# Three transformer layers on one core: a thin output projection two groups to a bank, and a second block with its values first

## What is computed

```python
# first block, after its first attention and residual:
h = rms_norm(x, norm_xattn);  m = rms_norm(mem, norm_mem)
q = (h @ xattn_wq)            # 4 heads of 128
s = softmax(q k^T / sqrt(128));  o = s v                # k, v from m
x = x + o @ xattn_wo          # 512 -> 2048: only 4 k-tiles of 128
h = rms_norm(x, norm_mlp)
x = x + square(relu(h @ w_up)) @ w_down
# second block, for l in range(2):
h = rmsnorm(x, norm_mix)
proj = h @ w_in               # qa ka va | qb kb vb | qc kc vc
oa = window_attention(qa, ka, va, sink, t5_table)       # 8 heads of 64
ob = neighborhood_attention(qb, kb, vb, b_rpb)          # 8 heads of 64, a bias and a mask
oc = axial_global_attention(qc, kc, vc, gains)          # 16 heads of 64, rotary
mix = concat(rmsnorm(oa), rmsnorm(ob), rmsnorm(oc))
x = x + mix @ w_o
h = rmsnorm(x, norm_mlp)
x = x + square(relu(h @ w_up)) @ w_down
```

## Time and profile before

| | |
|---|---|
| median of 3 runs | 3400.99 us (3398.97 to 3401.2) |
| the profiled execution | 3402.23 us, its span 3400.4 us |
| mean granted TensorE clock | 0.993 |
| PE busy | 98% of the span |
| DVE, ACT, POOL busy | 63%, 48%, 28% |

### The profile page before, as it was taken

One profiled execution on the slowest core, in us unless ns is written; L12 is line 12 of the kernel. 1 busy time (PEld: TensorE's weight loads), 2 busy tenths in 40 slices (PEclk: granted clock), 3 DMA queues, 4 the chain that ended last, 5 costly groups with the idle time before them and its releaser, 6 DMA issues.

```text
span 3400.4 us, 49070 instructions
## 1 busy us (share of the span) xinstructions
PE 3328.1 (98%) x19306; PEld 2885.9 (85%) x19306; DVE 2144.3 (63%) x3029; ACT 1635.9 (48%) x2755; POOL 948.4 (28%) x891
## 2 busy tenths in 40 slices
PE   8999998999999999999999999999999999999998
PEld 7888787888888887788888888888788888888887
DVE  5657566664576556777775467655777776457654
ACT  4455454443444544555444344444654544344443
POOL 1433132220132223246321023222336422013222
PEclk9999999999999999999999999999999999999999
DMA  6544453755555553465555555555354555555554
GB/s 215 194 152 143 138 172 131 251 191 197 184 189 191 190 189 127 140 177 165 186 184 188 193 186 191 194 186 175 122 172 158 186 186 188 196 186 188 197 186 142
DMA packets 187276, 605.58 MB, mean 178 GB/s; under 512 B 36485, under 2 KB 41461, under 8 KB 187046
## 3 DMA queue, kind: packets, MB, share of 16 engines
q1 hardware_dynamic: 187046, 602.44, 53.6%
HBM read 600.13 MB, written 8.00 MB: 179 GB/s over the span
## 4 chain that ended last, share of the span: by engine, by line
PE 88%; DVE 5%; ACT 4%; issue 1%; POOL 1%; DMA 0%; SPq 0%; POOLq 0%; DVEq 0%; ACTq 0%
PE ps L1591 87%; DVE wl L2171 3%; ACT wh L1926 2%; PE ps L1594 1%; DVE sS L2175 1%; ACT sS L2022 1%; ACT tA L1926 0%; ACT x L1926 0%; ACT sS L2011 0%; ACT sS L1988 0%; POOL acc L2505 0%; POOL sS L2505 0%; ACT tS L1931 0%; ACT ua L1926 0%; DVE den L2313 0%
## 5 line engine op out<-in xcount | busy, mean ns | idle before, releaser
L1591 PE MATMUL ps<-x,wh 128*128 128x512 f32 x4880 | 1735.1, 399 | 18.5 <-DVE x L2179 13.8
L2171 DVE TENSOR_TENSOR wl<-wt,wh 128x1024 fp32r<-128x1024 f32 x1098 | 1453.4, 1357 | 281.7 <-ACT wh L1926 266.8
L1591 PE MATMUL ps<-x,wl 128*128 128x256 f32 x4880 | 1370.9, 281 | 0.0
L1926 ACT ACTIVATE wh<-wt 128x1024 fp32r<-128x1024 f32 x1098 | 1108.2, 1052 | 173.4 <-PE ps L1591 162.6
L1591 PEld LDWEIGHTS ps<-x,wh 128*128 128x128 f32 x4880 | 919.6, 188 | 237.2 <-DVE wl L2171 14.7
L1591 PEld LDWEIGHTS ps<-x,wl 128*128 128x128 f32 x4880 | 925.9, 190 | 0.4
L1591 PE MATMUL ps<-ua,wh 128*128 128x512 f32 (+1 forms) x2432 | 844.2, 392 | 20.2 <-DVE xr L2171 9.3
L2171 DVE TENSOR_TENSOR tB<-ps,tA 128x256 f32<-128x256 f32 x497 | 208.8, 423 | 845.5 <-ACT tA L1926 843.6
L1926 ACT ACTIVATE tA<-ps 128x256 f32<-128x256 f32 x497 | 188.1, 382 | 1071.7 <-PE ps L1591 1062.7
L1591 PE MATMUL ps<-ua,wl 128*128 128x256 f32 x2368 | 666.1, 281 | 0.0
L1591 PEld LDWEIGHTS ps<-ua,wh 128*128 128x128 f32 x2432 | 455.0, 189 | 124.7 <-issue 10.0
(11 more groups left out here) (231 smaller groups left out, 1659.4 us busy)
## 6 DMA issues: line engine op xcount, KB each, us to landing
wt<-in_w_up SPq DMA_DIRECT2D x384, 512.0 KB, 3.9
wt<-in_w_down SPq DMA_DIRECT2D x384, 512.0 KB, 4.5
wt<-in_w_in SPq DMA_DIRECT2D x202, 512.0 KB, 4.4
wt<-in_w_o SPq DMA_DIRECT2D x64, 512.0 KB, 4.2
wt<-in_w_out SPq DMA_DIRECT2D x32, 512.0 KB, 4.2
wt<-in_wkv SPq DMA_DIRECT2D x16, 512.0 KB, 4.3
wt<-in_cw SPq DMA_DIRECT2D x8, 512.0 KB, 4.6
wt<-in_wq SPq DMA_DIRECT2D x8, 512.0 KB, 4.4
```

The costliest lines, as they stand in the source:

```text
L1591: return eng.matmul(o, l, r, start=start, stop=stop, skip_group_check=True)
L1926: return eng.activation(o, i, ACT.Copy, **kw)
L2171: return eng.tensor_tensor(o, a, b, op)
```

## The change

1. In the thin projection a group holds two outputs, one in each half of a bank: 4 groups of 4 tiles to a unit in place of 8 of 2. DVE adds 128x512 to two outputs of `xr` at once (`x = xr[:, o:o + 2, :]`), and `more` runs for both behind it.
2. `unit` gets `stages`, the values of `n` at which the background goes on: (3, 10, 15) and (7, 13) in the last two units of `xattn_wq`, (8, 13) and (4, 11) in the units of the thin projection.
3. In the second block vc comes before kc, and within B the order is qb, kb, vb. B's pairs are started together with A's. A pair waits for its values before their product, no longer before the scores. A takes slots 8 to 11 and B 12 to 15 (the rows of `w_o` are swapped on the host).
4. The factors of C's norm come at `n == 3` of the second unit of `w_o` (`across`), not right behind the first; until then evictions are held.

```diff
-ORDER2 = [26, 27, 28, 29] + [18 + i for i in range(8)] + [4, 5, 0, 1, 2, 3] + [6 + i + 4 * j for i in range(4) for j in (2, 0, 1)]
+ORDER2 = [28, 29, 26, 27] + [18 + i for i in range(8)] + [4, 5, 0, 1, 2, 3] + [6 + i + 4 * j for i in range(4) for j in range(3)]
...
-                if n == 8:
+                if n in stages:
                     run_deferred()
                     step_bg()
...
-    def at_once(begin, end):
+    def across(begin, end):
         kept = {}
 
         def first():
             kept["b"] = begin()
+            held["evac"] = True
+
+        def second():
+            end(kept["b"])
+            held["evac"] = False
+            run_pending()
         at13.append(first)
-        after_unit.append(lambda: end(kept["b"]))
+        after_unit.append(lambda: at3.append(second))
...
-        while (held["s1"] >= 1 or dens.spare() < 4 or not has("a_v", *v) or not (bias or sS.spare() >= 2)
+        while (held["s1"] >= 1 or dens.spare() < 4 or not (bias or sS.spare() >= 2)
...
+        while not has("a_v", *v):
+            yield
         av_heads(pr, [(hds[j], pts[j], j, v) for j in range(2)])
...
-        last_q = unit([(True, True, project("yq", i, "Q", free="yqfree"))], KT, X2)
+        last_q = unit([(True, True, project("yq", i, "Q", free="yqfree"))], KT, X2,
+                      stages=((8,), (8,), (3, 10, 15), (7, 13))[i])
...
-            last_p = unit([(True, True, residual("mlp", 8 * u + g, part == 1, G_MLP, thin=True, x2free=[last_q],
-                                                 last=(lambda: norm_T("mlp")) if 8 * u + g == 15 else None))
-                           for g in range(8)], 2, UA(2 * part), thin=True)
+            last_p = unit([(True, True, residual("mlp", 8 * u + 2 * g, part == 1, G_MLP, thin=True, x2free=[last_q],
+                                                 last=(lambda: norm_T("mlp")) if 8 * u + 2 * g == 14 else None))
+                           for g in range(4)], 4, UA(2 * part), thin=True, stages=(4, 11) if u else (8, 13))
...
-            slot = {"C": i, "B": 8 + i, "A": 12 + i}[br]
+            slot = {"C": i, "A": 8 + i, "B": 12 + i}[br]
...
-            elif 6 <= t < 10:
-                pair("B", t - 6)
             elif t == 5:
-                for i in range(4):
-                    pair("A", i)
+                for br in "AB":
+                    for i in range(4):
+                        pair(br, i)
...
-        gens = [spawn(branch("B", 1, 8)), spawn(branch("A", 2, 12))]
+        gens = [spawn(branch("A", 2, 8)), spawn(branch("B", 1, 12))]
...
-        at_once(lambda l=l: norm_begin((l, "C"), "accs0", "branch"), branch_end)
+        across(lambda l=l: norm_begin((l, "C"), "accs0", "branch"), branch_end)
...
-                    tt(xr[:, o, :], xr[:, o, :], ps[:, g % 3, 0:T], ALU.add).then_inc(S.v_sum)
+                    x = xr[:, o:o + 2, :]
+                    tt(x, x, ps[:, g % 3, :].rearrange("p (a b) -> p a b", a=2), ALU.add).then_inc(S.v_sum)
```

More of the change, by code:

```diff
@@ L249, in matmuls, with unit @@
             step("mm", h, k, k + 1)
-    def unit(parts, nk, src, thin=False):
+    def unit(parts, nk, src, thin=False, stages=(8,)):
         u = state["u"]
@@ L277, in unit @@
                 end = last and k == nk - 1
-                tiles[h].append((g, src(j, k), first and k == 0, end, thin))
+                if thin:
+                    half = 2 * k // nk
+                    tiles[h].append((g, src(j, k % (nk // 2)), k % (nk // 2) == 0, end, half))
+                else:
+                    tiles[h].append((g, src(j, k), first and k == 0, end, None))
                 matmuls(h, n % 8)
@@ L442, in ev @@
         def ev(g):
-            take("xw%d" % o, "xw", g)
+            os = (o, o + 1) if thin else (o,)
+            for i in os:
+                take("xw%d" % i, "xw", g, i)
             if thin:
@@ L455, in ev, with both, more @@
                 give(("tB", b), t)
-            give("xw%d" % o, t)
+            for i in os:
+                give("xw%d" % i, t)
             if not final:
                 return None
[L460 to L482, removed]
+            if thin:
+                def both():
+                    more(o, t)
+                    more(o + 1, t)
+                return both
+            return lambda: more(o, t)
+        def more(o, t):
+            step("more", st, o, nxt, fold)
+            p.free[("xw", st, o)] = [t]
+            if nxt is not None:
+                p.free[("x2", st, o)] = x2free
+                tick("a_x2hi", st, o)
+                tick("v_x2", st, o)
+                give("xr_split%d" % o, ("v_x2", at["v_x2", st, o]))
+            if fold:
+                take("rM", "rM", st, o)
+                square(st, o, "fold")
+            if o == 0:
+                take("acc", "acc", st)
+            if o == KT - 1 and not fold:
+                take("tS", "tS", st, o)
+                tick("a_sq", st, o)
+            else:
+                square(st, o)
+            if nxt is None:
+                give("xw%d" % o, tick("a_fin", o))
+            if last and o == KT - 1:
+                last()
         return ev
@@ L1599, in weights @@
                 for k in range(k0, k1):
-                    g, (src, i, key), start, end, thin = tiles[h][k]
+                    g, (src, i, key), start, end, half = tiles[h][k]
                     bank, c = ps[:, g % 3, :], slice(k * P, (k + 1) * P)
-                    if start:
+                    if start and not half:
                         let_go(w, "bank", g)
@@ L1609, in weights @@
                         x = U2(i)
-                    if thin:
-                        mm(bank[:, 0:T], wh[h % 4][:, c], x[:, 0:T], start, False)
-                        mm(bank[:, 0:T], wh[h % 4][:, c], x[:, T:2 * T], False, False)
-                        m = mm(bank[:, 0:T], wl[h % 4][:, c], x[:, 0:T], False, end)
+                    if half is not None:
+                        o = bank[:, half * T:half * T + T]
+                        stop = tiles[h][k][3] or k < 7 and tiles[h][k + 1][2]
+                        mm(o, wh[h % 4][:, c], x[:, 0:T], start, False)
+                        mm(o, wh[h % 4][:, c], x[:, T:2 * T], False, False)
+                        m = mm(o, wl[h % 4][:, c], x[:, 0:T], False, stop)
                     else:
@@ L2358, in _ @@
                     w.wait_ge(by_name[name], n)
-                    let_go(w, "xw", g)
-                    tt(xr[:, o, :], xr[:, o, :], ps[:, g % 3, 0:T], ALU.add).then_inc(S.v_sum)
+                    let_go(w, "xw", g, o)
+                    let_go(w, "xw", g, o + 1)
+                    x = xr[:, o:o + 2, :]
+                    tt(x, x, ps[:, g % 3, :].rearrange("p (a b) -> p a b", a=2), ALU.add).then_inc(S.v_sum)
                 elif kind == "memsplit":
```

4 lines of the change are left out of this document (2 added, 2 removed).

## The result

The changed kernel takes 3386.59 us (median of 5 runs, 3385.87 to 3390.24) against 3398.97 for the kernel before beside it (5 runs, 3393.34 to 3401.2): a ratio of 0.9967, interval 0.9953 to 0.9982. It is faster, by 12.4 us where 21.4 were forecast.

The account below looks back on a forecast made before the run. PE bounds the kernel (busy 3328.1 of 3400.4 us), so time comes off only its waits and low clock. Gains 5.3 + 3.6 + 7.9 + 4.6 = 21.4 give 3380; range 3376 to 3385, chance 0.60.

Parts of the forecast that it names:

- rivals A: Last thin part keeps most of its time: part 1's net gain nil, `w_up` stall 2 longer, about 3386; chance 0.15.
- rival B: Clock falls elsewhere, at `vturn` or in `w_o`, so the 5.1 credited to it is lost: 3385; chance 0.12.
- Part 0, 5.3: Head steps between `xattn_wq` matmuls: 4.7 of waits and 0.9 of slowed starts go, 0.3 charged; gain 5.3.
- Part 1, 3.6 net: Thin projection, two outputs a bank: 18.4 against 22.9, gain 4.5, minus 0.9 in the first unit of `w_up`.
- The bound on the squares: POOL's sums of squares beside DVE's splits in the thin projection: up to 3 us if POOL held ACT; not summed.
- Second block, the heads of both layers: Stalls of 1.72 and 1.77 in layer 0, 1.0 and 0.9 in layer 1 go; 0.5 added for vc's copy.
- The clock term of 3.4: Second block, layer 0: low clock of two windows, 1300 to 1310 and the ten us behind, removed: 2 x 1.7.
- 5.1 us credited to the clock: Second block, both layers: low clock goes with the gaps of 1.7 us, called a guess about cause; 5.1.
- The additions of layer 1: Second block, layer 1: the same three charges as layer 0 (0.5, 0.4, 0.9), given as 1.9 in all.
- one more case in which a turn stands right behind another pair's turn: Second block: a further late `sP`, as at 1438.12 where it came 1.26 late; charged 0.9.
- Rival D: Slower: PE waits on B's masks, 3.90 each, eight in full 31.2, giving 3411; chance 0.02.
- The removal of the `ua` waits: Before `w_o`: 2.0 in layer 0, 2.1 in layer 1 go through C's factors at `n == 3` and B's later-read slots.

Follow-up runs that it names:

- second_only: The kernel before with only the second block's plan of the change (parts 3 and 4): ratio 0.9994 (0.9986 to 1.0003) to the kernel before.
- b_spawn_old: The changed kernel with B's pairs started one by one with their own query unit, as before: ratio 0.9989 (0.9978 to 1.0000) to the kernel before.

## Why the prediction was right, and where it was not

**The sign and the range** were right; the size was 1.7 times too large. The 3386.6 lies outside the 3376 to 3385 that had 0.60, where rivals A and B stand (3386 and 3385). A did not come: the last part of the projection took 18.36 us for 18.4 forecast. B did, as told below.

**Part 0, 5.3.** The sum up to `w_up` was right (9.8 forecast, 10.6 measured), and so were its stages: 5.95 in `xattn_wq` and part 0 (5.3 forecast), 4.7 in part 1 (4.5 forecast). Which edit gives what was not. The term took all 4.7 us of waits for the head steps. 2.6 of them waited for `xr`, and those went with the longer evictions: part 2 is worth 2.8, part 1 of the change 7.8.

**Part 1, 3.6 net.** The cadence of 2.36, the wait of 3.76 before the last group (forecast: about 4), the low clock behind it and the stall in `w_up` all came. In `w_up` the price depends on when `sink` lands: 1.4 and 2.1 against 0.9. The unit took 11.6 us as forecast (11.4), but before it had taken 9.4, not 10.5. The wait for `x` in it was put at about 4; it was 1.90 in one execution and 4.44 in the other.

**The bound on the squares** was in the right place: DVE's low halves take 0.62 each where they took 0.51, and the squares' one buffer paces bunched outputs. No wait of PE names it, but ACT waits for POOL's sum nine times between 529 and 551 us, 0.43 to 1.12 each, where before it waited twice in that part (0.95 and 0.83). Before the add that frees the last group's bank (`xr<-xr,ps` at 536.89) DVE waits 0.20 and 0.60 for ACT's halves, so that up to 0.8 us of the 3.76 is this:

```profile
535.06 0.66 DVE L2203 SCALAR_TENSOR_TENSOR x<-xr,par,x 128x256 fp32r<-128x256 f32 x1 [0.20 <-ACT x L1950]
536.32 0.65 DVE L2203 SCALAR_TENSOR_TENSOR x<-xr,par,x 128x256 fp32r<-128x256 f32 x1 [0.60 <-ACT x L1950]
536.89 0.68 DVE L2195 TENSOR_TENSOR xr<-xr,ps 128x512 f32<-128x512 f32 x1
```

**Second block, the heads of both layers.** 1.72, 1.77, 1.0 and 0.9 of waits went, and 0.56 for the copy of vc came, as forecast. The clock term of 3.4 was half a guess: the dip at 1300 went and in both executions of the changed kernel one came near 1270 to 1280, behind waits of 0.95 and 0.85 that the kernel before has too. In five of the ten other executions with the new order of kc and vc there was none, and the stretch took 186.8 to 186.9, the 5.7 us of gain (6.4 forecast). Both executions with the old order had two dips there. Over the whole second block, up to the end of its second `w_o`, the kernel before has 10.2 us at half the clock (three dips of 3.4), the changed kernel 10.2 in one execution and 6.8 in the other. So of the 5.1 us credited to the clock none came in the first execution and 1.7 in the second. That was rival B. (The additions of layer 1, "1.9 in all", are 1.8 by their three terms, which moves nothing.)

**Second block, B and `w_o`.** This is, with the clock, the step that failed: "one more case in which a turn stands right behind another pair's turn [...] say 0.9". It came, in both layers, at 2.68, and with the clock's dip the unit is 3.4 us too long (12.45 against 9.07 in layer 0; the stretch of layer 1's last seven units 56.00 against 52.60). The stall of 1.26 from which 0.9 was taken is one of A, with no mask; B's mask lengthens DVE's splits beside it (3.40 against 2.37). The prediction weighed DVE's splits beside POOL's work for the squares, and did not ask it of the masks, one of which the new order puts ahead of such a turn's copy. Rival D had the masks as a wait of PE for POOL; that never came. They cost through DVE.

**`w_o`** has two waits for a bank, 1.9 us, in which two evictions stand behind two splits and the work on a branch's slots of `ua`; only 0.4 was charged. They are there without part 4 too, and in the kernel before one of 0.32 stood in their place. The removal of the `ua` waits was right, the reason wrong: they stay away without the factors at `n == 3` and without the swap of slots. They also stay away without B's early start, where a wait of 3.0 for B's `den` comes first. Which piece removes them was not shown; what the runs show is that the early start saves that wait of 3.0.

The missing 9.6 us (21.4 less 11.8 in the first execution) are then: 3.0 in layer 0 and 4.1 in layer 1 for B and `w_o`, 2.3 and 0.5 in the heads, 0.5 in `w_up`, less 0.8 gained above forecast. These numbers hold the 5.1 us of the clock. What part of a dip comes by chance is open: two executions of one kernel differ by 2.8 us in one stretch.

## What to carry to other kernels

Between a turn and its partner there must be more work than the copy's own engines have in their queues: count what stands ahead of the copy on ACT, and what DVE must do before that, in that unit, not in the one where such a stall was last seen. A new order moves the small steps between the products too: ask of each, a mask here, whether it comes to lie beside DVE's two-input work. And where outputs are bunched, look for the single buffer (`tS` here) that ties three engines into one cadence. Last, before a term is credited to the clock, look at more than one execution: here the dips came back elsewhere.

## What the hardware showed

PE ran full-clock stretches without waits at one of two tile rates, 0.347 or 0.353 us for two matmuls (5.55 or 5.65 us a unit), in the long stretches constant from the second unit on. Which one was drawn anew in each execution: the last 27 units of the first `w_up` took 149.8 in five and 152.6 in nine of 14 profiled executions, the second block's 179.2 or 182.4 (182.6 in one execution). What chooses the rate was not tried.

The start of the program also varies, from 295.0 to 301.9 us, but that is the clock: its dips there add up to 6.8 us at half speed in the shortest and 20.5 in the longest. With half of the dips' time taken off, all 14 lie between 291.3 and 292.4. Taken together, the five stretches that no kernel here changes (the start, the rest up to `xattn_wq`, the last 27 units of the first `w_up`, and the second block's two `w_up`) took 974.1 to 988.1 us, a spread larger than what this change gives. The runs of the kernel before lay between 3390.7 and 3405.8 (over all comparisons), about as far apart, and this is why stretches are the better measure here.

The wait for `sP` and the dips behind it go together, but not one for one. In 16 places (eight executions, two layers) the turn waited 2.1 to 2.7 us, and in 10 of them a dip of 3.4 us at half speed followed; in the 8 places where the wait was 0.52 to 0.84 none did. But a wait of 2.17 was followed by a dip (`second_only`, layer 1) and one of 2.68 was not (`b_spawn_old`, layer 0):

```profile
2517.24 1.02 PE L1602 MATMUL ps<-idt,sS 128*128 128x128 f32 x4 [2.17 <-ACT sP L1934]
```

```profile
2515.00:2520.00 5.00, 2.83 (x13) 2.50 (x12) 4.41 (x12) 2.09 (x3) 0.72 (x1) 0.73 0.36 126
```

```profile
1469.87 0.63 PE L1617 MATMUL ps<-idt,sS 128*128 128x128 f32 x4 [2.68 <-ACT sP L1951]
```

```profile
1470.00:1475.00 5.00, 5.00 (x31) 4.44 (x31) 4.19 (x16) 2.34 (x10) 0.00 (x0) 1.00 0.64 210
```

The first two views are of `second_only`, the last two of `b_spawn_old`: PE's timeline, and a window around or behind it. No length of wait in these runs separates the two.
